# Block boundaries of a two-layer encoder step: two chunks lead, the third joins later, squares of h summed by ones

## The reference, cut to what matters

```python
def rmsnorm(x, g):
    y = x * lax.rsqrt(jnp.mean(x * x, axis=-1, keepdims=True) + RMS_EPS)
    return y * g
def pre_mod(h, g_pre, shift, scale):
    return rmsnorm(h, g_pre) * (1 + scale[:, None, :]) + shift[:, None, :]
def post_add(h, y, g_post, gate, weight):
    return h + weight * gate[:, None, :] * rmsnorm(y, g_post)
def swiglu(x, w1, w2):
    g, u = jnp.split(x @ w1, 2, axis=-1)
    return (jax.nn.silu(g) * u) @ w2
# per layer, for the 512 prompt and the 64 sample tokens:
#   FFN 1:  h = post_add(h, swiglu(pre_mod(h, ...)), weight 0.5)
#   mixer:  x = pre_mod(h); P = x @ W_in; band attention, forgetting attention, spatial gating
#           m = sig(gA)*(oA@W_a) + sig(gB)*(oB@W_b) + sig(gC)*(oC@W_c)
#           h = post_add(h, m @ W_out, weight 1)
#   FFN 2:  as FFN 1
```

## Time and profile before

| | us |
|---|---|
| median of 3 runs | 2968.09 |
| lowest and highest | 2965.6, 2970.09 |
| the profiled execution's own time | 2967.36 |
| span of the profiled execution | 2965.6 |

### The profile page before, as it was taken

One profiled execution on the slowest core, in us unless ns is written; L12 is line 12 of the kernel. 1 busy time (PEld: TensorE's weight loads), 2 busy tenths in 40 slices (PEclk: granted clock), 3 DMA queues, 4 the chain that ended last, 5 costly groups with the idle time before them and its releaser, 6 DMA issues.

```text
span 2965.6 us, 49972 instructions
## 1 busy us (share of the span) xinstructions
PE 2851.5 (96%) x21582; PEld 2663.0 (90%) x21582; DVE 1341.4 (45%) x2606; ACT 988.4 (33%) x1861; POOL 108.6 (4%) x202
## 2 busy tenths in 40 slices
PE   7999998999999989999999999989999999999997
PEld 6999998877799989999989999987768999899997
DVE  3444325555444464443274443265554444644423
ACT  4222224344422352222252222244443224422321
POOL 0000000000000000000000000001000000000000
PEclk9999999999999999999999999999999999999998
DMA  5444432333222224442224444323321222122221
GB/s 228 149 150 156 166 107 96 105 108 100 81 86 79 86 79 143 155 143 84 86 86 144 161 159 151 98 84 120 122 94 55 82 81 83 65 86 79 90 82 65
DMA packets 91051, 324.28 MB, mean 109 GB/s; under 512 B 11200, under 2 KB 14304, under 8 KB 90640
## 3 DMA queue, kind: packets, MB, share of 16 engines
q1 hardware_dynamic: 64016, 222.50, 23.2%
q0 software_dynamic: 26816, 98.59, 9.7%
...
## 4 chain that ended last, share of the span: by engine, by line
PE 86%; DVE 6%; ACT 4%; issue 1%; DVEq 1%; DMA 1%; SPq 1%; POOL 0%; ACTq 0%
PE ps L613 76%; PE ps L919 3%; PE ps L703 2%; PE ps L932 1%; PE ps L952 1%; DVE h L1533 1%; DVE w_lo L1408 1%; ACT w_hi L1041 1%; DVEq L1532 1%; DMA w_raw<-in_f 1%; DVE x_lo L1540 1%; DVE z L1531 1%; PE ps L622 1%; ACT x_hi L1125 1%; ACT sig L1353 1%
## 5 line engine op out<-in xcount | busy, mean ns | idle before, releaser
L613 PE MATMUL ps<-x_hi,w_hi 128*128 128x290 f32 (+1 forms) x4256 | 980.4, 305 | 55.7 <-DVE x_lo L1540 37.8
L613 PE MATMUL ps<-x_lo,w_hi 128*128 128x288 f32 (+1 forms) x4256 | 949.5, 298 | 0.0
L613 PE MATMUL ps<-x_hi,w_lo 128*128 128x290 f32 (+1 forms) x4256 | 938.7, 295 | 0.0
L613 PEld LDWEIGHTS ps<-x_hi,w_hi 128*128 128x128 f32 x4256 | 691.1, 189 | 149.6 <-issue 93.8
L613 PEld LDWEIGHTS ps<-x_lo,w_hi 128*128 128x128 f32 x4256 | 701.3, 190 | 0.4
L613 PEld LDWEIGHTS ps<-x_hi,w_lo 128*128 128x128 f32 x4256 | 700.5, 190 | 0.0
L1408 DVE TENSOR_TENSOR w_lo<-w_raw,w_hi 128x1024 fp32r<-128x1024 f32 x386 | 469.5, 1223 | 264.9 <-ACT w_hi L1041 262.8
L1041 ACT CAST w_hi<-w_raw 128x1024 fp32r<-128x1024 f32 x386 | 393.5, 1048 | 98.9 <-DMA w_raw<-in_f 94.6
L613 PE MATMUL ps<-hid_hi,w_hi 128*128 128x288 f32 x1344 | 304.2, 297 | 1.8 <-DVE c_col L1465 1.8
L613 PE MATMUL ps<-hid_hi,w_lo 128*128 128x288 f32 x1344 | 301.9, 295 | 0.0
L613 PE MATMUL ps<-hid_lo,w_hi 128*128 128x288 f32 x1344 | 301.8, 295 | 0.0
...
## 6 DMA issues: line engine op xcount, KB each, us to landing
...
ada_w<-in_ada POOLq DMA_DIRECT2D x128, 512.0 KB, 5.7
...
```

The lines of the kernel that those rows point to most:

```text
L613: r = mm(ps[:, 2 * out + b, 0:width], w, xx[:, cols(b)], start=first and n == 0, stop=last and n == 2)
```

## The change

PE: `first_group` begins half 0 with chunks 0 and 1 for k = 0 and 1; chunk 2 joins, and the three go on together. `sum_of_y` of half 1 stands behind k = 2. Half 1 takes the three chunks together, k by k. The squares of h are summed by 16 ones matmuls into pair 3, one per tile and half, spread over the group; DVE's additions fall away. An FFN's chunk 3 is a whole chunk behind the group, in pair 1, and DVE takes it from PSUM. In out, three tiles instead of two are made by halves. ACT: the half 1 estimate stands behind k = 5 instead of 3, the squares and the late evictions are regrouped. Splits of ACT and DVE move, at the boundaries, in tri and at the kernel's start.

```diff
-OUT_PIECES = [(o, BOTH) for o in range(KD - 2)] + [(o, (b,)) for b in BOTH for o in (KD - 2, KD - 1)]
+
+LATE_SUMS = {3: (0, 1), 5: (2, 3), 7: (4, 5, 6, 7)}
+
+SQUARES = ({3: (0, 1, 2, 3), 5: (4, 5), 7: (6, 7)}, {1: (0, 1), 3: (2, 3), 5: (4, 5), 7: (6, 7)})
+OUT_HALVED = (KD - 3, KD - 2, KD - 1)
+OUT_PIECES = [(o, BOTH) for o in range(KD - 3)] + [(o, (b,)) for b in BOTH for o in OUT_HALVED]
...
-        def sum_of_h(l, j, p):
-
-            pe.wait_ge(h_summed.sem, h_summed.done(l, j))
-            for b in BOTH:
-                r = mm(pair[p][:, b, :], const[:, ONES, :], sum_h[:, columns(b)], start=True, stop=True)
-            r.then_inc(sum_h_ready.sem, 1)
-
-        def first_group(l, ph, n, lock, rest):
+        def sum_of_h(l, j, b, ks):
+
+            for k in ks:
+                pe.wait_ge(sq_h_ready.sem, sq_h_ready.done(l, x_index(j, b, k)))
+                r = mm(pair[3][:, b, :], const[:, ONES, :], sq_h[:, k, columns(b)], start=k == 0, stop=k == KD - 1)
+            if b and k == KD - 1:
+                r.then_inc(sum_h_ready.sem, 1)
+
+        def first_group(l, ph, n):
 
             j = (l, n - 1) if n else (l - 1, 2)
-            for s in lock:
+            first = (l, n) == (0, 0)
+
+            def some(b, group, ks):
+                for k in ks:
+                    pe.wait_ge(x_ready.sem, x_ready.done(l, x_index(n, b, k)))
+                    for s in group:
+                        r = x_half(l, ph, s, k, b)
+                        if b and k == KD - 1:
+                            r.then_inc(chunk_done.sem, 1)
+
+            for s in (0, 1):
                 chunk_ready(chunk(l, ph, s))
-                if s < 2:
-                    pair_free(l, ph, s, 0)
+
+            some(0, (0, 1), (0, 1))
+
+            chunk_ready(chunk(l, ph, 2))
+            some(0, (2,), (0, 1))
+            some(0, (0, 1, 2), (2,))
+            if not first:
+                sum_of_y(*j, 1)
+            some(0, (0, 1, 2), (3, 4, 5))
+
+            if not first:
+                sum_of_h(*j, 0, (0, 1))
+            some(0, (0, 1, 2), (6, 7))
+            if first:
+                first_ada(FIRST_MODS[1])
+                pe.wait_ge(start_shift.sem, start_shift.done(0, 0))
+            for s in (0, 1):
+                pair_free(l, ph, s, 0)
             for k in range(KD):
-                pe.wait_ge(x_ready.sem, x_ready.done(l, x_index(n, 0, k)))
-                for s in lock:
-                    x_half(l, ph, s, k, 0)
-                if k == 1 and j[0] >= 0:
-                    sum_of_y(*j, 1)
-            if (l, n) == (0, 0):
-                first_ada(FIRST_MODS[1])
-            for s in rest:
-                chunk_ready(chunk(l, ph, s))
-                for k in range(KD):
-                    x_half(l, ph, s, k, 0)
-            if (l, n) == (0, 0):
-                pe.wait_ge(start_shift.sem, start_shift.done(0, 0))
-            for group in ((0, 1), *((s,) for s in (*lock[2:], *rest))):
-                for k in range(KD):
-                    if group == (0, 1):
-                        pe.wait_ge(x_ready.sem, x_ready.done(l, x_index(n, 1, k)))
-                    for s in group:
-                        r = x_half(l, ph, s, k, 1)
-                        if k == KD - 1:
-                            r.then_inc(chunk_done.sem, 1)
+                some(1, (0, 1, 2), (k,))
+                if not first:
+                    if k + 2 < KD:
+                        sum_of_h(*j, 0, (k + 2,))
+                    if k in LATE_SUMS:
+                        sum_of_h(*j, 1, LATE_SUMS[k])
...
-            first_group(l, ph, n, (0, 1, 2), (3,))
-            if l or n:
-                pe.wait_ge(alt_taken.sem, alt_taken.done(l, ab == "b"))
-                sum_of_h(*((l, n - 1) if n else (l - 1, 2)), 2)
+            first_group(l, ph, n)
+            whole_chunk(l, ph, 3, 1, 1, x_hi, x_lo, moving)
             for i in range(2, KF):
-                for p in (0, 1) if i < KF - 1 else (0,):
-                    whole_chunk(l, ph, 2 * i + p, p, i - 1, x_hi, x_lo, moving)
-                if i == 2:
-                    pe.wait_ge(raw_taken.sem, raw_taken.done(l, 2 * (ab == "b")))
+                whole_chunk(l, ph, 2 * i, 0, i - 1, x_hi, x_lo, moving)
+                if i < KF - 1:
+                    whole_chunk(l, ph, 2 * i + 1, 1, i, x_hi, x_lo, moving)
...
-            for i in range(KD - 2):
-                whole_chunk(l, "out", i, i % 2, i // 2, m_hi, m_lo, columns,
+            for i in range(KD - 3):
+                whole_chunk(l, "out", i, *y_pair(1, i), m_hi, m_lo, columns,
                             gate=(lambda t: pe.wait_ge(prod_lo.sem, prod_lo.done(l, KF + t))) if i == 0 else None)
             for b in BOTH:
-                for i in (KD - 2, KD - 1):
-                    c = chunk(l, "out", i)
+                for i in OUT_HALVED:
+                    c, (p, group) = chunk(l, "out", i), y_pair(1, i)
                     if b == 0:
                         chunk_ready(c)
-                        pair_free(l, "out", i % 2, i // 2)
+                        if p < 2:
+                            pair_free(l, "out", p, group)
                     for k in range(KD):
-                        if b and i == KD - 2 and k == 4:
+                        if b and i == KD - 3 and k == 5:
                             sum_of_y(l, 1, 0)
...
-                            for p in pieces(j, 1):
-                                done(1, PIECES[j][p][0])
-                                evict(l, j, p)
-                        if k == 3:
+
+                        late = pieces(j, 1)
+                        if 0 <= k - 3 + len(late) < len(late):
+                            p = late[k - 3 + len(late)]
+                            done(1, PIECES[j][p][0])
+                            evict(l, j, p)
+                        if k == 5:
                             estimate(l, j, 1)
-                    if k > 3:
-                        square_h(l, j, b, k - 4)
-                for k in range(4, KD):
-                    square_h(l, j, b, k)
+                    for kk in SQUARES[b].get(k, ()):
+                        square_h(l, j, b, kk)
+                    if b == 0 and k in (5, 7):
+                        split_hi()
...
-                if s == 1:
-                    split_hi()
-            estimate_h(l, 0, 3)
+            estimate_h(l, 0)
+            split_hi()
...
-                if b == 0 and k in (3, 7):
-                    split_hi()
         act.wait_ge(ada_added.sem, ada_added.done(0, 1))
         high_shift(0, 0)
+
+        split_hi()
+        split_hi()
...
-                split_lo()
-                split_lo()
-                norm_of_h(*((l, 1) if ab == "b" else (l - 1, 2)), 2)
-            else:
-                split_lo()
-                split_lo()
+                norm_of_h(*((l, 1) if ab == "b" else (l - 1, 2)))
+            split_lo()
             for i in range(KF - 1):
-                if i < 2:
-                    first = (acc_free[0].sem, acc_free[0].done(l, GROUP_AT[ph][0])), (alt_taken.sem, alt_taken.done(l, ab == "b"))
-                    dve.wait_ge(*first[i])
-                    V.tensor_tensor(sil[:, i, :], sil[:, i, :], r2[:, :], ALU.mult).then_inc(g_scaled.sem, 1)
-                    first = (acc_free[1].sem, acc_free[1].done(l, GROUP_AT[ph][1])), (raw_taken.sem, raw_taken.done(l, 2 * (ab == "b")))
-                    dve.wait_ge(*first[i])
-                    V.tensor_tensor(hid[:, i, :], hid[:, i, :], r2[:, :], ALU.mult)
+                if i == 0:
+                    dve.wait_ge(acc_free[0].sem, acc_free[0].done(l, GROUP_AT[ph][0]))
+                    V.tensor_tensor(sil[:, 0, :], sil[:, 0, :], r2[:, :], ALU.mult).then_inc(g_scaled.sem, 1)
+                    dve.wait_ge(acc_free[1].sem, acc_free[1].done(l, GROUP_AT[ph][1]))
+                    V.tensor_tensor(hid[:, 0, :], hid[:, 0, :], r2[:, :], ALU.mult)
+                elif i == 1:
+                    dve.wait_ge(alt_taken.sem, alt_taken.done(l, ab == "b"))
+                    V.tensor_tensor(sil[:, 1, :], sil[:, 1, :], r2[:, :], ALU.mult).then_inc(g_scaled.sem, 1)
+                    split_lo()
+                    dve.wait_ge(chunk_done.sem, chunk_done.done(0, chunk(l, ph, 3)))
+                    take(hid[:, 1, :], 1, 3).then_inc(acc_free[1].sem, 1)
...
-            split_lo()
             dve.wait_ge(acc_free[1].sem, last_acc)
             new_h(l, j, 1, 0)
             new_h(l, j, 1, 1)
             x_low(nl, n, 1, 0)
             new_h(l, j, 1, 2)
             x_low(nl, n, 1, 1)
-            split_lo()
             x_low(nl, n, 1, 2)
...
-            add_squares_of_h(l, j)
+            split_lo()
+            split_lo()
...
+            norm_of_h(l, 0)
             split_lo()
-            norm_of_h(l, 0, 3)
...
-        for _ in range(LOOKAHEAD):
-            split_lo()
+        split_lo()
+        split_lo()
...
-                if b == 0 and k in (3, 7):
+                if (b, k) == (0, 1):
```

(58 more changed lines are left out.)

29 lines of the change are left out of this document (16 added, 13 removed).

## The result

The changed kernel takes 2946.51 us (median of 4 runs, 2943.5 to 2949.0), the kernel before 2968.88 (4 runs): ratio 0.9926, 95% interval 0.9909 to 0.9943, 22.4 us less. The forecast was 2945, range 2938 to 2957. The profiled execution took 2943.5 us with a span of 2941.7, 23.9 less than the span of before.

The account below looks back on a forecast made before the run. TensorE (PE) works 96% of the span, so the stake is its waits at five block boundaries and the start. Gains of 7.2 + 10.9 + 0.1 + 4.0 = 22.2 us off 2967.36 give 2945, range 2938 to 2957.

Parts of the forecast that it names:

- The boundary is counted from PE's instructions: Block boundaries: PE's time from y's last product to the squares' sum is its instructions (27.45 us) plus remaining waits (1.55).
- The price of the ones: Boundaries: each ones matmul costs PE 0.485 us, so 14 more add 6.8 us per boundary, 34 in five.
- Rival C: Among the products: a ones matmul costs more than 0.485, up to 0.96; 33 us more, 2978 us, chance 0.04.
- The x chain: DVE and ACT make x tile by tile at boundaries; half 1's last x_lo starts at 504.9 instead of 509.83.
- three causes: Half 1's last x_lo: moved ACT estimate wins 1.9 us, two low splits moved away 2.44, regrouped ACT squares 0.6.
- Rival A: Boundaries: half 1's last x_lo stays at 509.83 and only the ones are added; 17 us won, 2950, chance 0.13.
- Net by place: Gains: f2a to tri 7.2 us in two layers, out to f1b 10.9 in two, f2b to f1a 0.1, start 4.0.
- The third late tile at out: Out to f1b: one more tile evicted late, priced at 0.25 us against the gain there.
- The start: Kernel's start: half 0 takes 11.3 us instead of 15.75 as ACT's split moves behind x; net 4.0 us won.
- the 1.2 for an earlier begin: Kernel's start: one split fewer ahead of x lets it begin 1.2 us earlier.
- The clock: Behind tri's logits: the longer wait may bring the clock down, costing 1.5 us in each of both layers.
- Rival B: FFN starts: chunk 5 waits for pair 1 beyond 0.5 us of room; 2.5 us per us beyond, 2953, chance 0.08.

Follow-up runs that it names:

- e3: Changed kernel with the squares of h and the ones matrix rounded to the high format, so each ones matmul is one record: 2928.13 us.
- e2: Changed kernel with DVE adding the squares of h again and two ones matmuls behind the group summing them: 2948.49 us.
- e7: Changed kernel with out making its last two tiles by halves again, not three: 2951.3 us.
- e11: Changed kernel with DVE's third low split behind tri's scaled raw tiles instead of ahead of them: 2944.93 us.
- e1: The changed kernel run again unaltered, as the mark for the other runs: 2944.53 us, ratio 0.9927 to the kernel before.

## Why the prediction was right

*The boundary is counted from PE's instructions.* This step held. Forecast for f2a to tri: 29.0 us from the end of y to that of the sums (27.45 work, 1.55 waits). Measured: 480.74 to 507.68 + 1.94 = 509.62, 28.9. The waits foreseen at tile 6 and half 1's first tile (0.5 and 0.35) show as 0.35 and 0.24, which delay these tiles' first products by 0.52 and 0.40; the third, at half 1's second, is none, and some 0.3 us more in half 1's products and ones stand in its place. e3 shows that PE's own instructions bind, e2 that they may not simply be taken away.

*The price of the ones,* 0.485, is what the chain shows (1.94 for four). The Trainium skill, "Perfetto Trace Analysis", section "Engine Utilization", gives half the output rate for FP32_LOW_HIGH; the 0.24 us that the prediction estimated by it is what each record takes here (1.94 for eight), and a ones matmul is two of them. So the trace agrees with the page, and the prediction's estimate had left one record out. Rival C needed 0.8 and falls.

*The x chain.* The x_lo of its last two tiles are one row from 502.01 to 503.27; the last starts near 502.6, 22.0 us behind y's last product's start, for 26.45 before: 4.4 earlier, where 4.9 was forecast from three causes. Undone alone at this boundary, the estimate is worth 2.7 us and the splits 1.2. Rival A, in which the chain does not move, falls with that row.

*Net by place*, from the profiled executions (forecast in brackets): to the logits 3.89 and 3.88 (3.6 each); out to f1b, y's last product to the fifth chunk, 4.66 (5.45), and in layer 1, from the same product to the kernel's last one (2515.43 to 2945.99 before, 2497.51 to 2922.64 after), 5.4 (5.45); f2b to f1a 0.17 (0.1); start 2.8 (4.0). These are 20.8 of the 22.2 forecast. That the span fell by 23.9 is due to terms outside the sum, so that the sum's closeness is in part luck.

*Mis-sized terms.* (1) The third late tile at out: priced 0.25, it shows as the wait of 0.83 at tile 4 (1046.58), since DVE adds three late squares ahead of that tile's h and x (1.58 us, 0.45 for the one at f2a to tri).

(2) The start, 2.8 for 4.0. Half 0 took 11.0 us for the 11.3 foreseen: 1.5 above the 9.5 of its products, for the estimated 1.8 at half clock. What failed is the 1.2 for an earlier begin: PE began at 30.14, for 30.05 before, and the first ada product stands at 41.18, not near 40. In this execution PE's first sum, that of the squares of the input, took 10.80 us for 9.60, though both began alike (10.68 and 10.64); why isn't shown. But an earlier begin won nothing either. PE's timeline in e7, which began 1.24 us sooner, and the same window of the first profile and of e7:

```profile
28.90 0.58 PE L622 MATMUL ps<-x_hi,w_hi 128*128 128x288 f32 x1 [3.60 <-DVE x_lo L1554]
...
46.34 0.40 PE L622 MATMUL ps<-x_hi,w_hi 128*128 128x290 f32 x1 [0.74 <-DVEq L1933]
```

```profile
28.90:34.50 5.60, 4.36 (x23) 4.39 (x24) 5.60 (x12) 5.60 (x18) 0.00 (x0) 0.70 1.02 421
28.90:34.50 5.60, 5.60 (x24) 5.60 (x25) 5.60 (x15) 5.42 (x18) 0.00 (x0) 0.53 1.03 422
```

e7 is one record ahead at 34.50, since its granted clock was lower there, and its half 1 begins at 46.34 for 46.57. e2 (28.97 and 46.51) and e11 (29.25 and 46.85) are alike.

(3) Left out of the sum: the 1.4 us at half clock behind layer 1's logits, which the profiled execution after does not have; I had counted that place as a risk alone. The remaining 1.7 us of the 23.9 lie between the logits and out's last product (0.5 in layer 0 and 0.3 in layer 1), in layer 1's first FFN (0.4) and behind the kernel's last product (0.55), and are not explained.

*The clock* was thus a larger share than the text made plain: some 2.5 at each out to f1b and 1.4 behind the logits, 6.4 us of 23.9. The Trainium skill, "TensorE: Matmul & The Clock Gate", section "Why this matters for your kernels", asks to avoid the longer idle gaps between bursts; the 4.41 us gaps agree. The logits' waits are shorter, and there the runs differ: the 2.89 us, which the prediction held against the change, cost the clock in e1 and not in the first profile.

*Rival B* (pair 1): the unbroken 144 products show that it did not happen. DVE's take from pair 1 ends at 1082.41, and PE comes to chunk 5 at 1083.2: 0.8 us of room, for the 0.5 worked out.
